# A hybrid diffusion trunk, attention stage: the outputs of key tile kt are made behind the scores of tile kt+1 in place of tile kt+2

## The reference

```python
def block_attention(q, k, v):
    ...
    def one_block(qi):
        s = jnp.einsum('bqhd,bkhd->bhqk', qi, k).astype(jnp.float32) * ATTN_SCALE
        p = jax.nn.softmax(s, axis=-1)
        return jnp.einsum('bhqk,bkhd->bqhd', p.astype(v.dtype), v)
...
    q = (cq @ w_uq).reshape(B, L, N_HEADS_B, QK_DIM)
...
    kv = (keys_c @ w_ukv).reshape(B, Lk, N_HEADS_B, NOPE_DIM + V_DIM)
...
    o_b = block_attention(q, k, v).reshape(B, L, D_B)
```

## Time and profile before

| | |
|---|---|
| median of 3 runs | 1440.71 us (1439.24 to 1441.28) |
| the profiled execution, its time | 1439.18 us |
| its span | 1437.1 us |
| PE busy | 1334.8 us, 93% of the span, 6690 instructions |
| DVE busy | 706.4 us, 49% |
| ACT busy | 405.2 us, 28% |
| POOL busy | 225.7 us, 16% |
| the chain that ended last, by engine | PE 70%, DVE 15%, issue 5%, DMA 3%, POOL 3%, ACT 2% |
| mean granted TensorE clock | 0.97 |

### The profile page before, as it was taken

One profiled execution on the slowest core, in us unless ns is written; L12 is line 12 of the kernel. 1 busy time (PEld: TensorE's weight loads), 2 busy tenths in 40 slices (PEclk: granted clock), 3 DMA queues, 4 the chain that ended last, 5 costly groups with the idle time before them and its releaser, 6 DMA issues.

```text
span 1437.1 us, 17448 instructions
## 1 busy us (share of the span) xinstructions
PE 1334.8 (93%) x6690; PEld 1031.5 (72%) x6690; DVE 706.4 (49%) x1012; ACT 405.2 (28%) x715; POOL 225.7 (16%) x163
## 2 busy tenths in 40 slices
PE   6798999999999989889999999989999999996997
PEld 2697999999972436654444444468899999995886
DVE  4712323231414398876777887754423332224543
ACT  2712122121213122233333333525532111112321
POOL 1310000000003200034445544710000000000000
PEclk9798999999989999999999999999999999998999
DMA  8401242333241011500000000122221100013411
GB/s 366 139 16 34 88 152 100 139 118 121 104 171 41 15 47 63 197 14 6 1 22 6 22 0 0 32 79 88 88 72 47 31 31 31 31 31 117 176 44 59
DMA packets 29917, 105.68 MB, mean 74 GB/s; under 512 B 3659, under 2 KB 7951, under 8 KB 26544
## 3 DMA queue, kind: packets, MB, share of 16 engines
q1 hardware_dynamic: 28144, 97.98, 19.2%
q10 hardware_dynamic: 1728, 7.08, 1.3%
HBM read 88.35 MB, written 16.66 MB: 73 GB/s over the span
## 4 chain that ended last, share of the span: by engine, by line
PE 70%; DVE 15%; issue 5%; DMA 3%; POOL 3%; ACT 2%; SPq 0%; DVEq 0%; PEld 0%; POOLq 0%; ACTq 0%; PEldq 0%
PE bank L547 40%; PE bank L1016 13%; DVE amax_part L1752 3%; PE bank L874 2%; PE bank L901 2%; PE bank L770 2%; POOL fw L2040 2%; DMA SCR<-x_sample_in 2%; DVE amax_part L1754 2%; DVE SCR L1723 1%; PE bank L1075 1%; PE bank L706 1%; PE bank L558 1%; DVE SCR L1786 1%; PE bank L714 1%
## 5 line engine op out<-in xcount | busy, mean ns | idle before, releaser
L547 PE MATMUL bank<-H_r,WR_r 128*128 128x384 f32 x1728 | 353.8, 337 | 1.7 <-DVE H_r L1923 1.2
L547 PEld LDWEIGHTS bank<-H_r,WR_r 128*128 128x128 f32 x1728 | 303.3, 188 | 7.0 <-issue 4.8
L547 PE MATMUL bank<-H_r,SCR_r 128*128 128x384 f32 x480 | 161.0, 335 | 0.0
L2040 POOL TENSOR_TENSOR fw<-fw,SCR 128x1024 f32<-128x1024 f32 x56 | 142.0, 2536 | 92.0 <-ACT SCR L1369 90.8
L1369 ACT ACTIVATE SCR<-bank 128x512 f32<-128x512 f32 x144 | 82.9, 597 | 138.3 <-PE bank L874 129.9
L1016 PE MATMUL bank<-H_r,WR_r 128*128 128x512 f32 x432 | 100.0, 394 | 10.6 <-DVE SCR L1968 10.6
L2004 POOL TENSOR_SCALAR ssq<-ssq 128x1 f32<-128x1 f32 (+1 forms) x36 | 15.4, 429 | 575.7 <-ACT bank L1109 476.9
L547 PE MATMUL bank<-H_r,WX_r 128*128 128x384 f32 x384 | 99.8, 341 | 3.3 <-PEq L646 3.3
L1016 PEld LDWEIGHTS bank<-H_r,WR_r 128*128 128x128 f32 x432 | 82.4, 191 | 28.0 <-DVE SCR L1968 10.8
L1545 DVE SCALAR_TENSOR_TENSOR SCR<-bank,col,SCR 128x766 f32<-128x766 f32 (+1 forms) x96 | 43.0, 511 | 107.3 <-ACT SCR L1255 105.8
L547 PEld LDWEIGHTS bank<-H_r,SCR_r 128*128 128x128 f32 x480 | 90.5, 189 | 0.0
(11 more groups left out here) (303 smaller groups left out, 2114.5 us busy)
## 6 DMA issues: line engine op xcount, KB each, us to landing
WR<-w_mod_in SPq DMA_DIRECT2D x16, 1024.0 KB, 7.0
SCR<-w_in_in SPq DMA_DIRECT2D x20, 512.0 KB, 3.3
H<-w_mod_in SPq DMA_DIRECT2D x4, 2048.0 KB, 14.1
SCR<-x_sample_in SPq DMA_DIRECT2D x16, 512.0 KB, 14.5
WR<-w_io_in SPq DMA_DIRECT2D x16, 512.0 KB, 3.5
sp_rows<-SCR SPq DMA_DIRECT2D x9, 512.0 KB, 2.6
KV<-sp_rows SPq DMA_DIRECT2D x9, 512.0 KB, 6.8
H<-w_oe_in SPq DMA_DIRECT2D x2, 2048.0 KB, 12.7
```

The source lines that it names most:

```text
L547: last = nc.tensor.matmul(out, l, r, start=(n == 0), stop=(n == len(pairs) - 1))
L2040: ptt(p_acc, pT[0] if kt == 1 else p_acc, pT[kt % 3], ALU.add).then_inc(p_added, 1)
```

## The change

In `attend` on PE each call of `outputs` stands one step earlier. `outputs(i, s, 0)` comes behind `scores(i, s, 1)`, ahead of q1 and q2; in the loop over kt from 2 to 8 `outputs(i, s, kt - 1)` stands where `outputs(i, s, kt - 2)` stood; the call behind the loop, of tile 7, is gone. `outputs` of tile 8 keeps its place behind the first scores of the next head.

```diff
@@ -923,6 +923,7 @@
                 if after:
                     project(i, n, "kA", "kB")
                 scores(i, s, 1)
+                outputs(i, s, 0)
                 if after:
                     project(i, n, "q1", "q2")
                 for kt in range(2, KT9):
@@ -931,7 +932,7 @@
                         max_scores(i, n, 2 * kt - 6)
                     if kt == 7:
                         prompt_scores(i, s)
-                    outputs(i, s, kt - 2)
+                    outputs(i, s, kt - 1)
                     if kt == 8:
                         prompt_outputs(i, s)
                     if after:
@@ -939,7 +940,6 @@
                             max_scores(i, n, 2 * kt - 5)
                         if kt == 7:
                             max_rows_T(i, n)
-                outputs(i, s, KT9 - 2)
 
             project(0, 0, *STEPS)
             pe.wait_ge(i_done, CA)
```

## The result

The changed kernel takes 1468.26 us (median of 4 runs, 1463.67 to 1474.61) against 1440.99 for the kernel before: the ratio is 1.018, with a 95% interval of 1.014 to 1.023. The forecast of 1442.4 was wrong, and so was the range, which ended at 1448. The profiled execution has a time of 1463.67 and a span of 1461.6, 24.5 us more than before. The trace is of the fastest of the four runs; what made the two slowest 9 to 11 us longer still is in no trace.

A forecast was written before the change was run, and what follows sets the result against it. Each head was taken as DVE-bound for some 29 us and PE-bound for some 12 around the border. Six loop heads at +0.25 (+1.5) and the first head's +0.2 gave +1.7 on 1440.71: 1442.4 us, range 1437 to 1448.

The forecast's parts named there:

- The gain at the end: PE between last prompt matmul and next head's first score: 1.06 us shrinks to 0.20, gaining 0.86 a head (0.79 to 0.95).
- What it does to DVE: Mid-head: rotation add freed, first residue blocked by GpSimd's add, ending 1.11 us later; PE's hole before third maxima about 1.5.
- The sum without the clock: Per head: 1.11 us paid mid-head minus 0.86 gained at the end, +0.25 (bounds +0.05 to +0.41).
- the count of the drops: In the slow-clock rival: clock drops in three or four of the seven heads, +6 us on top of +1.7.
- the rival of the slow clock: Loop heads: the 1.5 us hole before the third maxima makes PE's clock fall; total 1448 us, chance 0.27.
- The price of one drop: Slow-clock rival: one drop of PE's clock costs 1.0 to 3.4 us, about 2.
- The first head: Attention's first head, on PE's pace mid-head, has the same two terms as the loop's heads: +0.2 us.
- The transfer of the row maxima: Negated maxima reach the next head's third score matmul with 0.29 us of cover left of 1.15; cost taken as 0.
- The first head's own drop goes: Rival: the first head's holes shift by 0.9 and its clock drop vanishes; at most -3.4 us, 1439.0, chance 0.12.
- The free middle: Rival: the moved pair only fills PE's mid-head holes, keeping 0.86 a head seven times; 1434.7 us, chance 0.14.

The follow-up runs named there:

- e1: Changed kernel plus six zero-weight matmuls on PE between the scores of key tile 4 and the third tile of maxima; 1444.28 us, ratio 1.001.
- e2: Changed kernel, GpSimd's add of key tile 3 also waits until the next head's first residue L1729 is done; 1432.64 us, ratio 0.992.
- e3: Changed kernel, on DVE the first residue L1729 stands ahead of the first reduction of maxima instead of behind the first reductions; 1430.69 us, ratio 0.992.
- e7: Changed kernel with three extra zero-weight matmuls at the place where e1 has six; 1446.66 us, ratio 1.004.
- e5: Kernel before with e2's edit alone: GpSimd's add of key tile 3 waits for the first residue L1729; 1437.08 us, ratio 0.997.
- e9: e3 with GpSimd's add of tile 2 held until the residue is done and that of tile 6 until DVE gated the earlier head's output; 1423.97 us, ratio 0.987.

## Why the prediction was wrong

- *The gain at the end* was 0.86: measured, 0.20 is left between the last prompt matmul (the second of two from 753.06, 0.11 apart) and the next scores at 753.37, as worked out.
- *What it does to DVE* held: the rotation add free (0.41), no hole before the first tile of maxima, the residue inside the add and 1.74 long (I had 1.6), and the hole of 1.62 before the third (I had 1.5).
- *The sum without the clock* was +0.25 a head; e1 has +0.37, inside the bounds. On 1440.7 I forecast 1442.4; e1, the changed kernel without the loop's drops, takes 1444.28 beside 1442.55 for the kernel before in the same runs: +1.7. That this is my sum to the tenth is luck: the interval of the ratio reaches from -1.7 to +4 us. The heads are the better evidence. Its six added matmuls stand in a hole, and none of their 1.5 us shows.
- *The step that failed is the count of the drops in the rival of the slow clock, and with it that rival's weight.* I named it with the right hole at the right place, gave it 0.27, and counted drops in "three or four of the seven heads". They came in all six heads of the loop, nine in all. The row of 0.51 behind a hole of 1.63 was the nearest one to a hole that I expected at 1.5, and should have been the likeliest case and not the second.
- *What the count lacked is what a drop does to the order of DVE and GpSimd*, although I had followed just that for the change. The price of one drop, 1.0 to 3.4 and about 2, was right: by the starts of the negations a short head of the changed kernel takes 839.48 - 796.64 = 42.8 us against 827.42 - 786.16 = 41.3 in e1, so its one drop costs 1.6. The long head takes 796.64 - 750.70 = 45.9 against 786.16 - 745.18 = 41.0, so its two drops with the blocked copy between them cost 5.0. That is 6.5 for two heads. From the second negation to the last, over the six heads of the loop, it is 267.6 against 248.3, so 19.3, where I had 6.
- *The first head* had +0.2 and took 40.5 instead of 39.5. The drop there lasts longer than before; the two were not taken apart.
- *The transfer of the row maxima* was taken at 0, rightly: the third matmul of the head at 753.37 starts 0.24 behind the second, without a wait.
- *The range* ended at 1448 because the slow clock was counted with a few drops; a case in which every head of the loop has one was not in it. The 1 us that I took as the spread between runs was small as well: 13 runs of the kernel before, made beside e1, lie between 1438.60 and 1449.39.
- *The first head's own drop goes*: it did not; the granted clock was 0.53 from 652 to 663, where before it was 0.51 from 652.4 to 659.2.
- *The free middle* is what e2 and e3 make real by a further edit: it needs the residue out of the add's way, as the rival said.

What stays open: why a hole of 0.93 with 0.50 behind it is followed by a drop in one head of e7 and not in the others, and why the same hole of 1.39 in the first head is followed by one in e5 and by none in e2 (clock 1.00 there). The runs show that it was so, not where the bound lies, and each kernel has only one trace.

## What to carry to other kernels

When an engine's work is moved within a pipeline, follow the others to the next place where DVE operations with two SBUF inputs, or copies, and GpSimd operations can meet: the stall rarely disappears, it picks another victim, and what it costs depends on what is queued behind that one. Where a new stall will leave PE idle in a dense stretch, look in the trace for any earlier hole of that size and what the granted clock did behind it, and take that row as the likeliest case; then follow the order at half clock too, since a drop moves the engines against each other and can make the next. The remedy is cheap here: one wait on the engine that has time to spare (e2) or a residue made earlier (e3) takes the changed kernel from 1.8% slower than the one before to 0.8% faster, and the earlier residue with two such waits to 1.3% faster (e9).

## What I had not expected of the hardware

- A plain copy of 128x640 from SBUF to SBUF on DVE (L1745), with one input, is blocked by GpSimd's add as well: 2.62 us instead of 0.48. The Trainium skill's page "SBUF — State Buffer", section "Who interferes with whom", names copies among those that can take the shared ports; the trace agrees.
- Who is first decides, even by less than 0.1 us: the copy started 0.08 behind an add, the rotation add before the change 0.07 behind one, and each stood until the add's end, over 2.1 us. The other way round GpSimd waits: in the kernel before, a gating instruction starts 0.16 ahead of an add and keeps its 0.67 us, and the add takes 2.74 instead of 2.36 (DVE's, then POOL's timeline):

```profile
775.09 0.67 DVE L1807 TENSOR_TENSOR H<-H,SCR 64x512 f32 x1
```

```profile
775.25 2.74 POOL L2040 TENSOR_TENSOR fw<-fw,SCR 128x1024 f32<-128x1024 f32 x1 [2.23 <-ACT SCR L1369]
```

- A fill of matmuls with zero weights, accumulated into a sum that is in use, kept the loop's granted clock at 1.00 (e1) where it was 0.90 without it, and its 1.50 us stood in time in which PE would have stood.
